# Trainium2, one core: projection passes handed from TensorE to ScalarE one token tile at a time, and a reordered start, in a hybrid RWKV-7 and gated-DeltaNet block

## Chip, cores and metric

The kernel runs on one core of one Trainium2 chip. The metric is the device time of one launch in microseconds (us). The engines are named as the profile names them: PE is TensorE, ACT is ScalarE, DVE is VectorE, POOL is GpSimd and SP is SyncE, which only issues DMAs here.

## What is computed

The layer works on x of 256 tokens by 2048 channels in float32. Its reference, cut to what matters:

```python
xn = rmsnorm(x, norm_mix_pre)
p = (xn @ w_in).astype(f32)
p_rwkv, p_qkv, p_z, p_beta, p_alpha, p_gate_a, p_gate_b = _split(p, IN_SPLITS)
# RWKV-7 branch: 32 heads x 64; its decay, its a and its gate come from three
# narrow ("LoRA") parts of p, 448 columns in all
y_a = (groupnorm(rwkv7_recurrence(...)) + bonus) * out_gate
# gated DeltaNet branch: 16 heads x 128, causal convolution, chunks of 64 frames
y_b = rmsnorm(gated_delta_rule_chunked(q, k, v, g, beta)) * silu(z)
mixed = sigmoid(p_gate_a) * y_a + sigmoid(p_gate_b) * y_b
x = x + rmsnorm(mixed @ w_out, norm_mix_post)
return x + rmsnorm((silu(xn2 @ ffn_w_gate) * (xn2 @ ffn_w_up)) @ ffn_w_down)
```

`w_in` has 2048 rows, and about 18,900 columns; all its products are needed in float32 accuracy.

## The kernel before

**Arithmetic.** Each large product is done in three matmuls: activations and weights are split into a high part that the matmul takes exactly and the rest. `product` issues hi x hi, lo x hi and hi x lo (L285 to L287). ACT makes the high part of a weight piece (`split_hi`, L275, tile `hi_all`), DVE the difference (`split_lo`, L280, tile `lo_all`). A piece of weights of 2 x 128 rows is called a quantum; four quanta are buffered (`QBUF`). PE says `quantum_done` at its end, and ACT may then overwrite the buffer.

**Stages.** The prologue turns x (8 groups of four transposes, L480, through PSUM to `xh` and `xl`, L490 and L500), and multiplies each group at once with the 480 LoRA and beta columns (`project_lora`, 16 quanta of 128 rows). Beside it ACT takes the squares for the first norm; its reciprocal root `rx` scales every accumulator that is emptied. Behind the projection stand the small steps for the LoRA parts, among the first splits of unit 0. Then come 16 units, one for each pair of RWKV heads and one DeltaNet head. A unit needs 24 quanta: three passes of eight quanta, each with 384 columns and all 16 row blocks, accumulated in PSUM banks 6 (tokens 0 to 127, tile 0) and 7 (tokens 128 to 255, tile 1). `take_out` (ACT, L311, tile `pu`) empties both banks, scaled by `rx`; then PE may begin the next pass, for which it waits for `pass_out`.

**Order of the work.** There is no scheduler. Each engine has a list that is written out by hand, and `fill(n)` puts the next n quanta (on ACT and DVE: their splits) between the steps of the recurrences. In a unit those steps are, in order: chunk work of the unit before, the small products for this one, then a triangular solve in levels (`LV`), each with a block Y and a block X of small 32-row matmuls (L984, tile `xs`, `yc`, `xi`), for which DVE prepares `yc` and `xi` (L1435). The passes of a unit begin behind chunk work, behind block X0 and behind block X4. Semaphores join the lists; an engine executes its list strictly in order.

**Last unit.** Instead of the next unit's projection the fillers are partial products with `w_out`: `out_hi`, `out_lo` (L375, L382), `out_part_pe` (L399 to L401, 344 or 336 columns, 7 quanta for a pass, six passes), emptied by `take_part` (L425, tile `keep`/`part`). Behind them the last two row blocks are added, then the output norm and the feed-forward stage (L530 to L546), which the change leaves alone.

## Time and profile before

| | |
|---|---|
| time before, median of 3 runs | 2151.61 us (2151.55 to 2154.91) |
| the profiled execution | 2157.32 us, its span 2155.6 us |
| mean granted clock of TensorE in it | 0.993 |
| PE busy | 2085.8 us, 97% |
| DVE busy | 1425.1 us, 66% |
| ACT busy | 1093.4 us, 51% |
| POOL busy | 160.4 us, 7% |

All rows below are of this one execution; its own time is the one to hold a sum of its durations against. In the page, a busy PE counts matmuls that overlap, so that a group's durations can add up to more than the stretch that they fill; the distance between the starts of two matmuls is their pace. "Idle before" in a timeline is the time in which the engine did nothing just before the row, with what ended it.

### The profile page before, as it was taken

What the parts mean: (1) busy time and instruction counts of PE and PEld (TensorE: products, weight loads), DVE (VectorE), ACT (ScalarE), POOL (GpSimd) and SP (SyncE); (2) the same over time, 40 slices, a digit from 0 to 9 for tenths busy, and PEclk for the clock granted to TensorE, in tenths of its full rate; (3) what the DMA queues carried; (4) which work ended last, traced back from release to release, by engine and by line L of the source; (5) the groups of instructions that cost most, each with busy time, mean ns of one, the idle gap of its engine ahead of it and who ended that gap; (6) DMA issues with size and microseconds to landing.
All of it is one profiled execution on the core that took longest, in us unless ns stands there. A gap on an engine that the chain in (4) does not pass through costs nothing. (4 is left out here: it accounts for less than half of the span.)

```text
span 2155.6 us, 49352 instructions
## 1 busy us (share of the span) xinstructions
PE 2085.8 (97%) x20516; PEld 1799.6 (83%) x20516; DVE 1425.1 (66%) x2865; ACT 1093.4 (51%) x2061; POOL 160.4 (7%) x277
## 2 busy tenths in 40 slices
PE   8999999999999999999999999799999999999998
PEld 7888888888888888888888888778888888888886
DVE  5668777777877877877787784764454544554446
ACT  5555554655655555465565554444444444444444
POOL 3001011011011101101101110000000000000000
PEclk9999999999999999999999999899999999999999
DMA  8654445544545444454444524555555555555543
GB/s 241 157 143 121 124 128 135 137 123 124 135 121 143 123 123 125 126 147 125 125 124 122 140 96 138 195 163 189 188 182 194 186 184 192 163 191 195 190 178 138
DMA packets 387773, 327.29 MB, mean 152 GB/s; under 512 B 11792, under 2 KB 334336, under 8 KB 381440
## 3 DMA queue, kind: packets, MB, share of 16 engines
q1 hardware_dynamic: 375792, 319.16, 50.5%
q10 hardware_dynamic: 11792, 5.42, 1.0%
q8 instruction: 142, 2.33, 0.5%
q14 instruction: 47, 0.39, 0.1%
HBM read 322.45 MB, written 2.10 MB: 151 GB/s over the span
## 5 line engine op out<-in xcount | busy, mean ns | idle before, releaser
L285 PE MATMUL ps<-hi_all,xh 128*128 128x384 f32 (+1 forms) x1568 | 562.6, 359 | 28.0 <-ACT pu L311 21.9
L534 DVE TENSOR_TENSOR lo_all<-stage,hi_all 128x1024 fp32r<-128x1024 f32 x263 | 322.1, 1225 | 366.4 <-ACT hi_all L530 366.0
L287 PE MATMUL ps<-hi_all,xl 128*128 128x384 f32 (+1 forms) x1568 | 530.1, 338 | 0.0
L286 PE MATMUL ps<-lo_all,xh 128*128 128x384 f32 (+1 forms) x1568 | 528.6, 337 | 0.0
L530 ACT ACTIVATE hi_all<-stage 128x1024 fp32r<-128x1024 f32 x260 | 275.4, 1060 | 402.4 <-PE ps L546 401.6
L280 DVE TENSOR_TENSOR lo_all<-stage,hi_all 128x768 fp32r<-128x768 f32 (+1 forms) x400 | 377.7, 965 | 117.0 <-ACT hi_all L275 116.3
L275 ACT ACTIVATE hi_all<-stage 128x768 fp32r<-128x768 f32 (+1 forms) x400 | 325.7, 833 | 196.2 <-PE ps L287 188.7
L285 PEld LDWEIGHTS ps<-hi_all,xh 128*128 128x128 f32 x1568 | 295.0, 188 | 63.6 <-issue 27.7
L286 PEld LDWEIGHTS ps<-lo_all,xh 128*128 128x128 f32 x1568 | 295.8, 189 | 0.8
L287 PEld LDWEIGHTS ps<-hi_all,xl 128*128 128x128 f32 x1568 | 295.3, 188 | 1.1
L542 PE MATMUL ps<-hi_all,xh 128*128 128x512 f32 x704 | 277.9, 395 | 5.2 <-DVE xl L500 5.2
L546 PE MATMUL ps<-hi_all,xl 128*128 128x512 f32 x704 | 276.6, 393 | 0.0
L544 PE MATMUL ps<-lo_all,xh 128*128 128x512 f32 x704 | 275.9, 392 | 0.0
L542 PEld LDWEIGHTS ps<-hi_all,xh 128*128 128x128 f32 x704 | 132.6, 188 | 42.5 <-DVE xl L500 6.8
L546 PEld LDWEIGHTS ps<-hi_all,xl 128*128 128x128 f32 x704 | 132.7, 188 | 29.1
L544 PEld LDWEIGHTS ps<-lo_all,xh 128*128 128x128 f32 x704 | 132.8, 189 | 23.4
L542 PE MATMUL ps<-hi_all,hh 128*128 128x512 f32 x348 | 137.8, 396 | 0.0
L544 PE MATMUL ps<-lo_all,hh 128*128 128x512 f32 x348 | 137.5, 395 | 0.0
L546 PE MATMUL ps<-hi_all,hl 128*128 128x512 f32 x348 | 137.4, 395 | 0.0
L1444 DVE SCALAR_TENSOR_TENSOR early<-ps,up,early 128x255 f32<-128x255 f32 (+1 forms) x192 | 83.2, 475 | 1.9
L984 PEld LDWEIGHTS ps<-late 128*64 128x64 f32 (+1 forms) x960 | 52.9, 135 | 32.2 <-issue 28.3
L542 PEld LDWEIGHTS ps<-hi_all,hh 128*128 128x128 f32 x348 | 65.2, 187 | 16.8 <-issue 0.9
(281 smaller groups left out, 2664.3 us busy)
## 6 DMA issues: line engine op xcount, KB each, us to landing
stage<-in_w_in SPq DMA_DIRECT2D x288, 512.0 KB, 5.7
stage<-in_ffn_w_gate SPq DMA_DIRECT2D x44, 1024.0 KB, 5.1
stage<-in_ffn_w_up SPq DMA_DIRECT2D x44, 1024.0 KB, 5.1
stage<-in_ffn_w_down SPq DMA_DIRECT2D x22, 2048.0 KB, 7.6
stage<-in_w_out SPq DMA_DIRECT2D x16, 344.0 KB, 4.3
stage<-in_w_out SPq DMA_DIRECT2D x8, 516.0 KB, 4.5
stage<-in_w_in SPq DMA_DIRECT2D x8, 448.0 KB, 6.3
stage<-in_w_out SPq DMA_DIRECT2D x8, 336.0 KB, 4.7
```

The source lines that it names most:

```text
L275: nc.scalar.activation(split_of(hi, u, q), raw_quantum(u, q), ACT.Copy).then_inc(hi_ready, 1)
L280: nc.vector.tensor_tensor(split_of(lo, u, q), raw_quantum(u, q), split_of(hi, u, q).bitcast(F32), ALU.subtract).then_inc(lo_ready, 1)
L285: nc.tensor.matmul(o, xh[:, kc, xs], high, start=kc == 0, stop=False)
L286: nc.tensor.matmul(o, xh[:, kc, xs], low, start=False, stop=False)
L287: return nc.tensor.matmul(o, xl[:, kc, xs], high, start=False, stop=kc == KC - 1)
L530: nc.scalar.activation(whi[b], src, ACT.Copy).then_inc(ffn_hi, 1)
L534: nc.vector.tensor_tensor(wlo[b], src, whi[b].bitcast(F32), ALU.subtract).then_inc(ffn_lo, 1)
L542: nc.tensor.matmul(o(t), left_hi[:, k, xs], whi[b][:, k, :], start=first and k == 0, stop=False, skip_group_check=True)
L544: nc.tensor.matmul(o(t), left_hi[:, k, xs], wlo[b][:, k, :], start=False, stop=False, skip_group_check=True)
L546: last = nc.tensor.matmul(o(t), left_lo[:, k, xs], whi[b][:, k, :], start=False, stop=False, skip_group_check=True)
L984: return nc.tensor.matmul(o, l, r, start=start, stop=stop, skip_group_check=True)
L1444: steps.step(name, nc.vector.scalar_tensor_tensor(o, x, s, y, op0, op1))
```

## The change

- **Token tile outside, row block inside.** `project` and `out_pe` had the row blocks (`k`) outside and the token tiles (`t`) inside. Now `t` is outside, so that in the last quantum of a pass bank 6 is complete six matmuls before bank 7. PE says so with a new semaphore, `bank_done`. `take_out` and `take_part` empty tile 0 behind `bank_done` and tile 1 behind `quantum_done`, and each of the two instructions adds one to `pass_out`. PE waits for tile 0's before the first matmul of the new pass and for tile 1's before the seventh.
- **Place of the take-outs.** Behind X0 (`i == 0`) the take-out stands ahead of a unit's `fill(before_y[0])` instead of behind it. `take_part` follows the split of quantum `n % OG == 1` instead of `== 2`. In unit 0, the take-out of pass 1 follows split 18 instead of 17.
- **Loads.** The first x load of 512 columns becomes two of 256, the first LoRA weights come in two halves with a semaphore `first_in`, and unit 0's first weights (`load_unit_weights(sp, 0, (0,))`) are issued ahead of `load_small`.
- **First norm.** Two squares of 2048 columns become eight of 512 (`sq0` to `sq7`), one ahead of each group's splits; DVE adds up the eight sums (`sum`).
- **Head of PE.** 24 transposes of the identity into bank 6 (`warm`, 10, 8 and 6) stand ahead of the first norm transpose, ahead of group 0's transposes and behind them. The transposes of group 1 follow quantum 0 and no longer precede it.
- **LoRA steps.** The steps behind the projection (`un`, `shift`, `tlw` and so on) stand at other places among unit 0's splits, and two quanta rather than four precede the LoRA transposes.

The diff, cut to its core:

```diff
--- before.py
+++ after.py
+WARM = (10, 8, 6)
...
-        def load_unit_weights(sp, u):
-            for i in range(6):
+        def load_unit_weights(sp, u, parts=range(6)):
+            for i in parts:
...
+        def landed(fill):
+            return 48 * (fill // 3 + 1) - (32 if fill % 3 == 0 else 0)
...
+        def taken(n, t):
+            return 2 + NT * n + t + 1
         def project(pe, u, q):
             j = q // 8
-            if q % 8 == 0 and not (isinstance(u, int) and u + j == 0):
-                pe.wait_ge(pass_out, 3 * u + (2 + j))
             pe.wait_ge(lo_ready, count(u, q + 1))
-            for k in range(2):
-                for t in range(NT):
+            for t in range(NT):
+                if q % 8 == 0 and u + j > 0:
+                    pe.wait_ge(pass_out, taken(3 * u + j - 1, t))
+                for k in range(2):
                     last = product(ps[:, 6 + t, 0:PW], 2 * (q % 8) + k, t, hi[q % QBUF][:, k, :], lo[q % QBUF][:, k, :])
+                if q % 8 == 7 and t == 0:
+                    last.then_inc(bank_done, 1)
             last.then_inc(quantum_done, 1)
...
             act.wait_ge(quantum_done, QALL + (n + 1 - QBUF))
             nc.scalar.activation(hi[n % QBUF][:, :, 0:OW[out_pass(n)]], out_quantum(n), ACT.Copy).then_inc(hi_ready, 1)
-            if n % OG == 2 and n > OG:
+            if n % OG == 1 and n > OG:
                 take_part(act, n // OG - 1)
...
         def take_out(act, u, j):
-            act.wait_ge(quantum_done, count(u, 8 * (j + 1)))
             for t in range(NT):
-                last = nc.scalar.activation(pu[:, t, (j % 3) * PW:(j % 3 + 1) * PW], ps[:, 6 + t, 0:PW], ACT.Copy,
-                                            scale=rx[:, t:t + 1])
-            last.then_inc(pass_out, 1)
-        def pass_columns(u, j):
-            return 3 * u + (3 + j)
+                if t == 0:
+                    act.wait_ge(bank_done, 3 * u + j + 1)
+                else:
+                    act.wait_ge(quantum_done, count(u, 8 * (j + 1)))
+                nc.scalar.activation(pu[:, t, (j % 3) * PW:(j % 3 + 1) * PW], ps[:, 6 + t, 0:PW], ACT.Copy,
+                                     scale=rx[:, t:t + 1]).then_inc(pass_out, 1)
...
         def take_part(act, p):
-            act.wait_ge(quantum_done, QALL + OG * (p + 1))
             b = part_bank(p)
-            nc.scalar.activation(part[:, :, OAT[p]:OAT[p] + OW[p]], ps[:, b:b + NT, 0:OW[p]], ACT.Copy).then_inc(pass_out, 1)
+            for t in range(NT):
+                if t == 0:
+                    act.wait_ge(bank_done, 3 * NU + p + 1)
+                else:
+                    act.wait_ge(quantum_done, QALL + OG * (p + 1))
+                nc.scalar.activation(part[:, t, OAT[p]:OAT[p] + OW[p]], ps[:, b + t, 0:OW[p]], ACT.Copy).then_inc(pass_out, 1)
...
                     load_x(0)
-                    for fill in range(4):
-                        if fill == 1:
-                            load_x(1)
-                        if fill == 2:
-                            load_x(2)
-                            load_x(3)
-                        if fill >= 3:
+                    load_low(0, 0, 2, 0, 448, first_in)
+                    load_low(0, 0, 4, 448, LW, first_in)
+                    load_x(1)
+                    load_low(0, 2, 4, 0, 448, weights_in[0])
+                    load_x(2)
+                    for fill in range(1, 4):
+                        if fill == 3:
                             load_rows()
                             sp.wait_ge(lo_ready, 4 * fill - 8)
-                        for at, col, n in ((0, COL_LORA, 224), (224, COL_LORA + 224, 224), (448, COL_BETA, 32)):
-                            to = raw[fill % 3].rearrange("p a b -> p (a b)")[:, 0:4 * LW]
-                            sp.dma_start(to.rearrange("p (k n) -> p k n", k=4)[:, :, at:at + n],
-                                         w_in3[:, 4 * fill:4 * fill + 4, col:col + n]
-                                         ).then_inc(weights_in[fill % 3], 16)
+                        for c1, c2 in ((0, 224), (224, 448), (448, LW)):
+                            load_low(fill, 0, 4, c1, c2, weights_in[fill % 3])
+                        if fill < 3:
+                            load_x(fill + 2)
+                    load_unit_weights(sp, 0, (0,))
                     load_small()
-                    load_unit_weights(sp, 0)
+                    load_unit_weights(sp, 0, range(1, 6))
...
+                    def squares(i):
+                        t, c = i % 2, i // 2
+                        act.wait_ge(x_in[max(c + 1, 1)], 16)
+                        if i >= 4:
+                            act.wait_ge(A.sem, A.after(f"sq{i - 4}"))
+                        cs = slice(512 * c, 512 * c + 512)
+                        A.step(f"sq{i}", nc.scalar.activation(junk[:, 512 * (i % 4):512 * (i % 4) + 512], xt[:, t, cs], ACT.Square,
+                                                              accum_out=ssc[:, t, c:c + 1]))
                     for g in G8:
                         if g == 0:
                             act.wait_ge(D_.sem, D_.after("n1"))
+                        else:
+                            squares(g - 1)
                         transpose_x_act(act, A, Pe, NORM1, (g,))
                         for q in (2 * g, 2 * g + 1):
                             split_hi(act, None, q)
-                        if g >= 6:
-                            squares(g - 6)
+                    squares(7)
                     for q in range(2):
...
+                    dve.wait_ge(A.sem, A.after("sq7"))
+                    step("sum", nc.vector.tensor_reduce(ss[:], ssc[:], AX.X, ALU.add))
+                    step("var", nc.vector.tensor_scalar(ss[:], ss[:], 1.0 / D, NORM_EPS, ALU.mult, ALU.add))
+                    root(nc, dve, D_, "rx", rx[:], ss[:], rt[:])
+                    for q in range(2):
+                        split_lo(dve, 0, q)
                     dve.wait_ge(small_in, 16 * N_SMALL)
                     for i, (_, n) in enumerate(lora_cols):
...
+                    def warm(n):
+                        for _ in range(n):
+                            nc.tensor.transpose(ps[:, 6, 0:P], ident[:], ident[:])
                     pe.wait_ge(masks_made, 3)
+                    warm(WARM[0])
...
+                    warm(WARM[1])
                     turn_x(0)
+                    warm(WARM[2])
                     for g in G8:
-                        if g + 1 < KC // 2:
+                        if 0 < g < KC // 2 - 1:
                             turn_x(g + 1)
                         for q in (2 * g, 2 * g + 1):
                             pe.wait_ge(D_.sem, D_.after(f"lo{g}"))
                             project_lora(pe, q)
+                            if q == 0:
+                                turn_x(1)
...
-                    for q in range(4):
+                    for q in range(2):
...
                 for i in LV:
+                    if i == 0 and more:
+                        take_out(act, u, 3)
                     fill(before_y[i])
                     if i == 4:
                         after(E, "Y4")
                         fn("yw", yw[:].rearrange("p a j -> p (a j)"), ps[:, 2, 0:6 * BK])
                     fill(before_x[i])
-                    if i == 0 and more:
-                        take_out(act, u, 3)
```

**First place: ACT at the pass that begins behind X0, in a steady unit.** `th` is the last step of the small products, `hi_all` a split, and `pu` the take-out. Before:

```order
L1300 ACTIVATE th<-pu 128x768
L275 ACTIVATE hi_all<-stage 128x768 [waits quantum_done,weights_in0] x2
L311 ACTIVATE pu<-ps,rx 128x384 [waits quantum_done]
L311 ACTIVATE pu<-ps,rx 128x384
L275 ACTIVATE hi_all<-stage 128x768 [waits quantum_done,weights_in0]
L275 ACTIVATE hi_all<-stage 128x768 [waits quantum_done,weights_in1] x4
```

and in the changed kernel:

```order
L1352 ACTIVATE th<-pu 128x768
L285 ACTIVATE hi_all<-stage 128x768 [waits quantum_done,weights_in0]
L330 ACTIVATE pu<-ps,rx 128x384 [waits bank_done]
L330 ACTIVATE pu<-ps,rx 128x384 [waits quantum_done]
L285 ACTIVATE hi_all<-stage 128x768 [waits quantum_done,weights_in0] x2
L285 ACTIVATE hi_all<-stage 128x768 [waits quantum_done,weights_in1] x4
```

The take-out now has one split ahead of it and not two, and its two instructions wait for two events, not for one.

**PE where such a pass begins,** in a unit of the changed kernel: the last small matmul ahead, then one quantum.

```order
L1036 MATMUL ps<-rhg,xit 64x128
L295 MATMUL ps<-hi_all,xh 128x384 [waits pass_out,lo_ready]
L296 MATMUL ps<-lo_all,xh 128x384
L297 MATMUL ps<-hi_all,xl 128x384
L295 MATMUL ps<-hi_all,xh 128x384
L296 MATMUL ps<-lo_all,xh 128x384
L297 MATMUL ps<-hi_all,xl 128x384
L295 MATMUL ps<-hi_all,xh 128x384 [waits pass_out]
L296 MATMUL ps<-lo_all,xh 128x384
L297 MATMUL ps<-hi_all,xl 128x384
L295 MATMUL ps<-hi_all,xh 128x384
L296 MATMUL ps<-lo_all,xh 128x384
L297 MATMUL ps<-hi_all,xl 128x384
```

Six matmuls on tile 0 stand between the two waits for `pass_out`. Before the change the first row carried the only wait, and the tiles alternated every three matmuls.

**Second place: ACT in the last unit, at the take-out of part 0** (`keep`), before:

```order
L375 ACTIVATE hi_all<-stage 128x2x344 [waits quantum_done,weights_in0] x2
L1300 ACTIVATE late<-ps,ege 128x128 [waits pe_front]
L1300 ACTIVATE late<-ps,ege 128x128
L1300 ACTIVATE late<-ps 128x256 [waits pool_front]
L1300 ACTIVATE late<-ps 64x2x64 x4
L1300 ACTIVATE late<-ps,uh 128x128 x2
L1300 ACTIVATE th<-pu 128x768
L563 DMA g2s<-in_rwkv_g 128x2x128 [waits pe_back]
L375 ACTIVATE hi_all<-stage 128x2x344 [waits quantum_done,weights_in0]
L425 ACTIVATE keep<-ps 128x2x344 [waits quantum_done]
```

and in the changed kernel:

```order
L389 ACTIVATE hi_all<-stage 128x2x344 [waits quantum_done,weights_in0] x2
L447 ACTIVATE keep<-ps 128x344 [waits bank_done]
L447 ACTIVATE keep<-ps 128x344 [waits quantum_done]
L1352 ACTIVATE late<-ps,ege 128x128 [waits pe_front]
L1352 ACTIVATE late<-ps,ege 128x128
L1352 ACTIVATE late<-ps 128x256 [waits pool_front]
L1352 ACTIVATE late<-ps 64x2x64 x4
L1352 ACTIVATE late<-ps,uh 128x128 x2
L1352 ACTIVATE th<-pu 128x768
L586 DMA g2s<-in_rwkv_g 128x2x128 [waits pe_back]
L389 ACTIVATE hi_all<-stage 128x2x344 [waits quantum_done,weights_in0]
```

The take-out has moved ahead of `late`, `th`, the issue of the load of `g2s`, and one split.

**Third place: PE's head**, before:

```order
L836 MATMUL ps<-ident,junk 128x16 [waits norm_in,masks_made]
L480 MATMUL ps<-ident,xt 128x128 [waits x_in0]
L480 MATMUL ps<-ident,xt 128x128 x7
L285 MATMUL ps<-hi_all,xh 128x480 [waits lo_ready,pre_dve]
L286 MATMUL ps<-lo_all,xh 128x480
L287 MATMUL ps<-hi_all,xl 128x480
L285 MATMUL ps<-hi_all,xh 128x480
L286 MATMUL ps<-lo_all,xh 128x480
L287 MATMUL ps<-hi_all,xl 128x480
```

and in the changed kernel:

```order
L879 MATMUL ps<-ident 128x128 [waits masks_made]
L879 MATMUL ps<-ident 128x128 x9
L884 MATMUL ps<-ident,junk 128x16 [waits norm_in]
L879 MATMUL ps<-ident 128x128 x8
L503 MATMUL ps<-ident,xt 128x128 [waits x_in0]
L503 MATMUL ps<-ident,xt 128x128 x3
L879 MATMUL ps<-ident 128x128 x6
L295 MATMUL ps<-hi_all,xh 128x480 [waits lo_ready,pre_dve]
L296 MATMUL ps<-lo_all,xh 128x480
L297 MATMUL ps<-hi_all,xl 128x480
L295 MATMUL ps<-hi_all,xh 128x480
L296 MATMUL ps<-lo_all,xh 128x480
L297 MATMUL ps<-hi_all,xl 128x480
L503 MATMUL ps<-ident,xt 128x128 [waits x_in1]
```

Fillers (L879, whose only input is the identity) stand ahead of and behind the norm's transpose, and once more behind the first group's; the other four transposes of the eight have moved behind quantum 0.

## Rows read from the trace of the kernel before

**Rows 1.** Windows, one unit: us, busy and (count) per engine, PEclk, DMA share, GB/s.
```profile
200.86:278.12 77.26, 75.53 (x1032) 66.95 (x1033) 59.52 (x146) 42.98 (x99) 8.93 (x13) 1.00 0.50 129
```

**Rows 2.** Waits of the whole span: us in total, times, longest us.
```profile
ACT hi_all L275 <- PE ps L287: 188.7, 129, 2.2
...
PE ps L285 <- ACT pu L311: 21.9, 32, 1.1
```

**Rows 3.** Timeline of PE at X0: start us, us, engine, line, operation, tiles, [idle before].
```profile
199.60 0.59 PE L984 MATMUL ps<-yc,xs 32*32 32x16 f32 x48
200.86 0.44 PE L285 MATMUL ps<-hi_all,xh 128*128 128x384 f32 x1 [0.66 <-ACT pu L311]
...
205.70 0.33 PE L287 MATMUL ps<-hi_all,xl 128*128 128x384 f32 x1
205.88 0.33 PE L285 MATMUL ps<-hi_all,xh 128*128 128x384 f32 x1
...
208.05 0.59 PE L984 MATMUL ps<-yc,xs 32*32 32x16 f32 x48
208.57 0.44 PE L285 MATMUL ps<-hi_all,xh 128*128 128x384 f32 x1
```

**Rows 4.** Timeline of ACT and of DVE in the same stretch.
```profile
199.04 0.83 ACT L275 ACTIVATE hi_all<-stage 128x768 fp32r<-128x768 f32 x1
199.78 1.03 ACT L311 ACTIVATE pu<-ps,rx 128x384 f32<-128x384 f32 x2
...
206.29 0.25 DVE L1435 TENSOR_TENSOR yc<-ps,lev 128x96 f32<-128x96 f32 x1
```

**Rows 5.** Timeline of PE behind X4 of the same unit.
```profile
224.49 0.45 PE L285 MATMUL ps<-hi_all,xh 128*128 128x384 f32 x1 [0.65 <-ACT pu L311]
```

**Rows 6.** Timeline of the head on PE, ACT; then windows of it (same columns as the unit).
```profile
5.37 1.97 PE L480 MATMUL ps<-ident,xt 128*128 128x128 f32 x8 [1.25 <-DMA xt<-in_x]
9.60 0.74 PE L285 MATMUL ps<-hi_all,xh 128*128 128x480 f32 x1 [2.26 <-DVE lo_all L280]
...
18.40 0.84 ACT L490 ACTIVATE xh<-ps,par 128x256 fp32r<-128x256 f32 x2 [1.21 <-PE ps L480]
...
9.60:15.08 5.48, 5.48 (x16) 4.53 (x17) 2.42 (x5) 1.36 (x4) 4.40 (x16) 1.00 1.08 379
15.08:18.12 3.04, 3.04 (x20) 2.65 (x18) 1.88 (x4) 1.83 (x4) 2.46 (x9) 1.00 0.80 234
19.27:20.71 1.44, 1.44 (x8) 1.26 (x7) 1.44 (x4) 0.95 (x2) 1.17 (x5) 1.00 0.27 35
```

**Rows 7.** Around 39 and 55 us: PE's waits (30:42, 50:60), ACT, SP, a window.
```profile
PE ps L285 <- DVE lo_all L280: 2.9, 2, 2.3
...
PE ps L285 <- DVE lo_all L280: 0.9, 2, 0.5
...
37.03 1.57 ACT L275 ACTIVATE hi_all<-stage 128x768 fp32r<-128x768 f32 x2 [1.90 <-DMA stage<-in_w_in]
...
26.60 0.43 SPq L248 DMA_DIRECT2D stage<-in_w_in  x1
...
38.80:42.20 3.40, 3.09 (x10) 3.12 (x11) 2.76 (x4) 2.37 (x4) 0.00 (x0) 0.50 1.01 280
```

**Rows 8.** Timeline of PE at the end of pass 0 of unit 0.
```profile
59.45 0.34 PE L287 MATMUL ps<-hi_all,xl 128*128 128x384 f32 x1
60.93 0.44 PE L285 MATMUL ps<-hi_all,xh 128*128 128x384 f32 x1 [1.14 <-ACT pu L311]
```

**Rows 9.** Last unit: window of ACT's work, timeline of ACT, of DVE.
```profile
1275.99:1279.18 3.19, 3.19 (x26) 2.90 (x26) 2.06 (x6) 3.09 (x11) 1.11 (x2) 1.00 0.93 330
...
1280.93 0.74 ACT L425 ACTIVATE keep<-ps 128x688 f32<-128x688 f32 x1 [0.97 <-PE ps L401]
...
1290.33 0.25 DVE L1435 TENSOR_TENSOR yc<-ps,lev 128x96 f32<-128x96 f32 x1
```

More of the change, by code:

```diff
@@ L389, in last_bank, with out_pe @@
             return (6, 0, 2)[p % 3]
-        def out_pe(pe, n, bank, kc0, first):
+        def out_pe(pe, n, bank, kc0, first, emptied=None, tell=False):
             pe.wait_ge(lo_ready, QALL + n + 1)
             w = OW[out_pass(n)]
-            for k in range(2):
-                kc = kc0 + k
-                for t in range(NT):
+            for t in range(NT):
+                if emptied is not None:
+                    pe.wait_ge(pass_out, taken(emptied, t))
+                for k in range(2):
+                    kc = kc0 + k
                     xs, o = slice(t * P, (t + 1) * P), ps[:, bank + t, 0:w]
@@ L401, in out_pe @@
                     last = nc.tensor.matmul(o, xl[:, kc, xs], h, start=False, stop=False, skip_group_check=True)
+                if tell and t == 0:
+                    last.then_inc(bank_done, 1)
             last.then_inc(quantum_done, 1)
@@ L865, in _ @@
                     Pe.step("lora", last)
[L866 removed]
+                    for q in range(2, FIRST):
                         project(pe, 0, q)
```

79 lines of the change are left out of this document (42 added, 37 removed).

## Prediction

> **What bounds the kernel now.** I read the busy shares first, then who waited for whom, then stretches of the timeline. TensorE (PE) is busy for 75.53 us of a unit of 77.26 us, VectorE (DVE) for 59.52, ScalarE (ACT) for 42.98, at the full granted clock [rows 1]. So PE sets the pace of the 16 units. ACT even waits 188.7 us in all for PE to free a split buffer [rows 2], which means that the weight splits run ahead. What PE loses there is mostly one wait: its first matmul of a pass waits for ACT to empty the two accumulators of the pass before, 21.9 us in 32 waits [rows 2]. Two of 1.14 us come before the units (the one at 60.93 [rows 8], and its like 18 us later); the other 30, 19.6 us, are two in each of 15 units: at the passes that begin behind the small blocks X0 and X4. The other parts of the change lie in the first 80 us, where PE stands still several times, and in the last unit with the output projection, where PE follows DVE.
>
> **Part 1, passes handed over by token tile, units 0 to 14.** At the first place the 48 small matmuls of X0 start at 199.60 and the pass at 200.86; behind the same block at 208.05 the next quantum starts at 208.57 [rows 3]. So 1.26 us stand against 0.52: 0.73 us are lost (0.66 idle, and 0.07 of overlap that a stopped PE does not have). ACT shows why: it splits from 199.04 to 199.8, begins the two evacuations at 199.78 when the old pass has just ended, and needs 1.03 us for both [rows 4]. At the second place the pass starts with 0.65 idle behind it [rows 5]; by the same overlap I take 0.71. After the change tile 0 is complete six matmuls (6 x 0.17 = 1.04 us) before the pass ends, so ACT can take it at once; its take-out has also been moved ahead of the split. It is free about 199.1, and empties tile 0 until 199.7, before X0 is over at 200.1. Tile 1 is complete at 199.7 and empty at about 200.3; PE wants it only after the new pass's first six matmuls, at 201.2. Both waits vanish: 15 x (0.73 + 0.71) = **-21.6 us**.
>
> What is late next: the split moved behind the take-out comes at about 200.3 instead of 199.04, and DVE's difference for it about 0.3 us later than now. DVE works in order, so `y1` at 206.29 [rows 4] becomes 206.6 to 206.85, and PE, now 0.73 earlier, asks for it at 207.3 (208.05 less 0.73). 0.4 us of slack remain, so the move costs nothing. The third hand-over of a unit lies behind chunk work and shows no wait now. One increment and one wait more per pass cost nothing that I can find: between 205.70, the last matmul of one quantum (with an increment), and 205.88, the first of the next (with a wait already met), lie 0.18 us, against 0.17 between any two [rows 3]. The Trainium skill (page TensorE: Matmul & The Clock Gate, section The cost: per-tile semaphore tail) speaks against this part: every increment on completion costs about 26 ns and they serialize, so one on the last matmul is better. By that figure some 54 more increments on TensorE would be an estimated 1.4 us against me, and the forecast a good 1 us later; the row's 0.01 us decides.
>
> **Part 2, the first 80 us.** Five things, in order of time.
> (a) Head. The first projection matmul starts at 9.60 and the next group at 15.08, 5.48 us for 16 instructions; no less work takes 3.04 from 15.08 to 18.12 [rows 6]. The granted clock reads 1.00 in both, but its first record in this trace comes only at 14.9; by the times, the first stretch ran at 1.2 GHz and the second at 2.4. The change fills the idle head with 24 transposes. If they bring the full clock by 9 us, the first group needs 2.6 to 3.0 us. But group 1's transposes now come behind quantum 0, and from their end ACT needs 0.84 and DVE, behind it, 1.44 [rows 6], less some overlap, so PE waits for that chain about 1.2 us. The first matmul itself I put at 9.3: x arrives earlier, but ahead of its transposes stand 18 fillers at the pace of the first transposes, 8 in 1.97 us [rows 6]. Group 1 then starts at about 13.4, **-1.6 us** (bounds 0 and -2.4).
> (b) Squares. ACT's two squares of 2,048 columns stand among the last groups' splits; of the 2.9 us that PE waits for DVE there in two waits [rows 7], the shorter one of about 0.5, at 34 us, is theirs, 0.7 lost with the overlap. In eight pieces they fit into the 1.21 us that ACT waits in a group [rows 6]: -0.7.
> (c) First pass. The longer wait, 2.3 us, ends at 39.1 [rows 7], 2.5 lost. DVE waits for a split that ACT can start only at 37.03, since its weights land late; SP issued them at 26.60, behind the small loads [rows 7]. Now they are issued ahead of those, about 6 us earlier, and should have landed long before. What remains is the norm: last square, sum, some ten small DVE operations of the root (0.2 us each, an estimate), one difference. By that I get 0.9 us idle: **-1.6**.
> (d) Clock. Behind that stop the granted clock is 0.50, 1.2 GHz, from 38.8 to 42.2 [rows 7], while PE does 10 matmuls in 3.09 us, 0.31 each where 0.17 is the pace at the full clock [rows 3]: some 1.5 us for what falls into it. With 0.9 us idle I expect no fall: **-1.5**.
> (e) The LoRA steps spread among the splits: PE waits 0.9 us for DVE in two places from 50 to 60 [rows 7], 1.3 with the overlap, and both go. The two pass ends ahead of the units (59.45 to 60.93 is 1.48 in place of 0.17 [rows 8]) cost 1.31 each and go as in part 1: -1.3 - 2.6.
> Together -1.6 - 0.7 - 1.6 - 1.5 - 1.3 - 2.6 = **-9.3 us** (bounds: -4 if (a), (c) and (d) give nothing, -11).
>
> **Part 3, last unit and output projection.** Here the change also costs. `take_part` follows `out_hi` one quantum earlier. For part 0 that puts it ahead of 3.19 us of ACT work (`late` to `th`, 11 instructions from 1275.99) [rows 9], and it must wait for the partial pass to end, which lets ACT evacuate at 1280.93 now [rows 9]. That work then starts at about 1281.4, after the evacuation (0.74 less what tile 0 had in advance); the splits behind it and the squares come 3 to 5 us late. DVE's differences wait for them, then its chain of small operations, then `y1`, which I put at 1292.75, 2.4 later than its 1290.33 [rows 9]; PE wants it at about 1291, by its own pace (an estimate, as is the rest of this part). I charge +2.2 and give back 0.3 for the pass's own wait: **+1.9**. Part 4's take-out now stands between two splits, not behind both, so DVE's last output chain starts about 1.2 later, and part 5's stands ahead of one more split that the last turned tile waits for: +1.2 and +0.6, near the length of one evacuation and of one split. Nothing hides these, as PE waits for DVE there already. Sum **+3.7 us** (bounds 0, if later work has slack, and +6, if the granted clock falls once more at (d)'s price). The feed-forward stage is untouched and PE-bound.
>
> **Sum.** -21.6 - 9.3 + 3.7 = -27.2 us, from the profiled execution's own 2157.3 (span 2155.6 and 1.7 around it): 2130.1. That execution is 5.7 above the median of the three timed runs; I take the saving off the median: 2151.6 - 27.2 = 2124.4, rounded **2124 us**.
>
> **Rivals.**
> - *Fillers do not raise the clock.* Now 8 transposes in 1.97 us from 5.37 [rows 6] left it low, which speaks for it; against it, PE stood still for 2.26 us behind them [rows 6], and the fillers leave no such gap. Then (a) gives nothing or 0.3: 2124.4 + 1.5 = 2126. Chance 0.25. The Trainium skill has that rule (page TensorE: Matmul & The Clock Gate, section Part 4: PE-mode transpose): the full clock does not engage for PE-mode transposes.
> - *ACT does not reach the second tile in time.* Tile 1's 0.57 us plus hand-over latency leave 0.3 us of room; if one of the two hand-overs per unit keeps its wait: + 15 x 0.7 = 2135. Chance 0.07.
> - *DVE binds as soon as PE's wait is gone.* DVE is busy 77% of a unit and its chains set X and Y. Then only part 2 stays: 2151.6 - 9.3 + 3.7 = 2146. Against it: DVE waits for ACT, and ACT for PE, all through. Chance 0.04. That is also the case in which the change does not do what it says.
> - *Slower.* ACT, in order, stands at `bank_done` ahead of the split in every unit as it does in the last one, the difference comes late, `y1` later, and PE waits at X1. It decides once the split is late by more than the 0.4 us of slack plus the 1.8 us a unit that the rest saves (27/15). At 3.2 us late, as in the last unit: (3.2 - 0.4) x 15 = +42, 2166. But ACT reaches the take-out at 199.04, after tile 0 is complete and 0.7 before tile 1 is. Chance 0.02.
>
> **How the numbers follow.** Forecast 0.62, with its own range 2118 to 2130 from the bounds of parts 2 and 3; the rivals 0.25, 0.07, 0.04, 0.02. The range 2115 to 2133 takes in the first rival, the bounds, and the 3.4 us between the timed runs; about 0.15 lie outside. A difference of 0.2% (4.3 us) is about what this kernel's runs can tell from none. Faster 0.96, same 0.02, slower 0.02.
>
> **What would show it.** In a unit of the new profile, no idle PE ahead of the pass behind X0 and behind X4, and units of 75.8 us instead of 77.26. In the head, matmuls 0.22 apart from the first on; no 0.50 clock near 39; the second pass's start at about 53 instead of 60.93. In the last unit, ACT idle ahead of its first `keep` evacuation and PE idle ahead of X1. The prediction is wrong if units keep a wait for `pu`, or if a wait for `lo_all` or `yc` takes its place.

## Result and profile after

The changed kernel takes 2129.24 us (median of 4 runs, 2128.61 to 2130.34) against 2153.26 us of the kernel before (4 runs, 2151.55 to 2155.59). The ratio is 0.9888, 95% interval 0.9871 to 0.9905: 24 us faster, where 27 were forecast. The time itself, 2129.24, is 5.2 us above the 2124 of the forecast: 3.2 of them are the smaller saving, and the rest is mostly the kernel before, whose median is 2153.26 here and was 2151.61 there. A later measurement of the same kernel on another chip (e11 below) gave 2127.04 against 2154.07, a ratio of 0.9878 (0.9862 to 0.9895).

The page and the whole span's waits of PE after the change (us in total, times, longest us):

```profile
span 2126.9 us, 49422 instructions
PE 2081.5 (98%) x20540; PEld 1798.8 (85%) x20540; DVE 1424.9 (67%) x2866; ACT 1097.5 (52%) x2079; POOL 160.8 (8%) x277
```
```profile
PE ps L1036 <- issue: 10.0, 20, 1.2
PE ps L503 <- DVE keep L2059: 6.5, 1, 6.5
PE ps L565 <- DVE xl L523: 5.2, 5, 2.1
PE ps L295 <- DVE lo_all L290: 3.9, 3, 2.0
PE ps L415 <- DVE xl L1325: 3.0, 1, 3.0
PE ps L415 <- DVE lo_all L396: 2.1, 2, 1.4
...
```

PE's wait for `pu` [rows 2] is not in the list any more; all 32 of them are gone. The first row, idle time of PE at the small blocks for which the profile names no releaser, was 7.3 us in 15 waits before. Most of it is 0.42 us at one later block of a unit, in both kernels at the same place (16.6 us behind the pass at X0); the largest new one is the 1.25 us in the last unit shown below. The unit reads like this now, as a window and at block X0, on PE and on ACT (columns as in rows 1 and 3):

```profile
191.56:267.34 75.78, 75.36 (x1041) 66.93 (x1033) 59.50 (x145) 43.17 (x99) 8.93 (x13) 1.00 0.51 131
```
```profile
191.04 0.59 PE L1036 MATMUL ps<-yc,xs 32*32 32x16 f32 x48
191.56 0.44 PE L295 MATMUL ps<-hi_all,xh 128*128 128x384 f32 x1
...
190.48 1.25 ACT L330 ACTIVATE pu<-ps,rx 128x384 f32<-128x384 f32 x2
```

From the start of X0 to the pass behind it 0.52 us go by, as at an ordinary quantum, where it was 1.26 [rows 3]. ACT takes the first tile at 190.48, ahead of X0, where it began as the old pass ended [rows 4]. A unit takes 75.78 us instead of 77.26 [rows 1]: 1.48 each.

The two traces can be laid side by side at the same instructions. The table shows how much earlier the changed kernel reaches each, by its start in either trace.

| reached | before | after | earlier by | in this stretch |
|---|---|---|---|---|
| quantum 2 of the LoRA projection | 15.08 | 15.23 | -0.15 | head (a): -0.15 |
| last LoRA quanta (group 7) | 33.95 | 33.54 | 0.41 | squares (b): 0.56 |
| first pass | 39.11 | 37.66 | 1.45 | first pass (c): 1.04 |
| second quantum of it | 42.70 | 39.84 | 2.86 | clock (d): 1.41 |
| second pass | 60.93 | 55.39 | 5.54 | LoRA steps and a hand-over (e): 2.68 |
| third pass | 79.01 | 72.06 | 6.95 | a hand-over: 1.41 |
| first output quantum behind the last take-out of a unit | 1256.97 | 1227.65 | 29.32 | 15 units: 22.4 |
| block Y4's quantum in the last unit | 1296.69 | 1269.42 | 27.27 | part 0's take-out: -2.05 |
| third output quantum behind it | 1306.10 | 1277.02 | 29.08 | a clock fall that only the trace of before has: 1.81 |
| last output quantum | 1383.41 | 1356.90 | 26.51 | parts 4 and 5: -2.57 |
| end | 2155.6 | 2126.9 | 28.7 | clock falls that lie otherwise: 1.25; gathered from 1400 to 1800 without a fall: 0.97 |

The two profiled executions lie 28.7 us apart, the medians 24.0. The clock of these two does not tell why in total: both have a mean granted clock of 0.993, and about 31 us at 0.50 each. What differs is where the falls lie. Two of the kernel before have no like in the other trace (3.4 us from 38.8 and from 1301.7), the changed kernel has one in the head (3.4 us from 9.5) and a longer one near 1344 (6.8 us, where the kernel before has 3.4), and the fall of 10.2 us behind the output projection is in both, but in the changed kernel more of it lies where PE stands idle (before, then after):

```profile
1390.50:1400.70 10.20, 7.95 (x24) 6.21 (x25) 7.41 (x17) 1.68 (x4) 0.00 (x0) 0.50 0.30 92
```
```profile
1361.20:1371.40 10.20, 5.05 (x15) 3.98 (x16) 9.56 (x33) 3.06 (x7) 0.00 (x0) 0.50 0.04 3
```

The trace alone with all these effects taken out says about 27 us. That is an estimate: 28.7, less 1.4, 1.8 and 1.25 for the falls that cost the kernel before more, plus 1.2 for the longer fall near 1344 and 1.7 for the one in the head (15.23 there, 13.54 in e11).

A median mixes executions of different clocks, and the time of one kernel follows its mean granted clock. Thirteen runs of the kernel before on one chip took 2149.94 to 2152.91 us at a mean clock of 0.995 or 0.996 (five runs), 2153.89 to 2156.50 at 0.993 or 0.994 (seven) and 2158.96 at 0.992. Held against each other at one clock, the two kernels lie 26 to 28 us apart at 0.993 (four of these runs, and the two of the changed kernel at 2128.61 and 2129.11, on another chip), and on e11's chip 24.4 to 26.4 at 0.994 and about 26.5 at 0.995. So the change is worth some 24 to 28 us, and the runs do not tell a 27 from a 25.

In the head, the transposes and the start of the projection, and the clock in two windows there:

```profile
4.29 1.94 PE L879 MATMUL ps<-ident 128*128 128x128 f32 x8
6.05 0.62 PE L503 MATMUL ps<-ident,xt 128*128 128x128 f32 x4
6.50 0.82 PE L879 MATMUL ps<-ident 128*128 128x128 f32 x6
9.30 0.58 PE L295 MATMUL ps<-hi_all,xh 128*128 128x480 f32 x1 [1.98 <-DVE lo_all L290]
...
15.23 0.45 PE L295 MATMUL ps<-hi_all,xh 128*128 128x480 f32 x1 [0.62 <-DVE lo_all L290]
```
```profile
6.00:9.00 3.00, 1.32 (x12) 1.08 (x10) 1.29 (x3) 2.23 (x5) 2.50 (x8) 1.00 1.01 353
9.50:12.50 3.00, 3.00 (x11) 2.49 (x10) 0.26 (x1) 0.00 (x0) 2.37 (x9) 0.50 1.12 372
```

Eight fillers take from 4.29 to 6.05, 0.22 us each; the four transposes behind them and the next fillers are 0.11 apart. So the full clock came at 6.0 us, by transposes alone, 8.9 us earlier than before (14.9). Then PE stood still for 1.98 us, and from 9.5 on the granted clock is 0.50 (1.2 GHz) for more than 3 us. The first six matmuls run at the low clock again, and in this execution nothing is won.

In the last unit, ACT at the take-out of part 0 and PE at block X1:

```profile
1250.66 0.46 ACT L447 ACTIVATE keep<-ps 128x344 f32<-128x344 f32 x1 [3.90 <-PE ps L417]
1251.61 0.46 ACT L447 ACTIVATE keep<-ps 128x344 f32<-128x344 f32 x1 [0.49 <-PE ps L417]
1251.96 0.62 ACT L1352 ACTIVATE late<-ps,ege 128x128 f32<-128x128 f32 x2
```
```profile
1262.97 0.58 PE L1036 MATMUL ps<-yc,xs 32*32 32x16 f32 x48 [1.25 <-issue]
```

ACT waits 3.90 us for the first tile, with `late` and `th` behind it in its list. They start at 1251.96; in the place that they had before [rows 9] they would have started at 1275.99 less 29.32, that is 1246.67. The price shows up 11 us later, where PE waits 1.25 us. That row names no releaser; that the wait comes from the take-out's place is shown by e3 below.

### The profile page after: what moved, and what is told of

Read it like the earlier page. It is cut to its first block and busy times, and to the rows that moved or that the text cites. A ratio compares the mean times of both kernels' runs of the same rounds, so it can differ in the third digit from the quotient of the medians.

```text
span 2126.9 us, 49422 instructions
## 1 busy us (share of the span) xinstructions
PE 2081.5 (98%) x20540; PEld 1798.8 (85%) x20540; DVE 1424.9 (67%) x2866; ACT 1097.5 (52%) x2079; POOL 160.8 (8%) x277
## 5 line engine op out<-in xcount | busy, mean ns | idle before, releaser
L295 PEld LDWEIGHTS ps<-hi_all,xh 128*128 128x128 f32 x1568 | 294.2, 188 | 36.1 <-issue 24.4
L569 PEld LDWEIGHTS ps<-hi_all,xl 128*128 128x128 f32 x704 | 132.4, 188 | 28.7
```

The lines of the kernel that those rows point to most:

```text
L295: nc.tensor.matmul(o, xh[:, kc, xs], high, start=kc == 0, stop=False)
L569: last = nc.tensor.matmul(o(t), left_lo[:, k, xs], whi[b][:, k, :], start=False, stop=False, skip_group_check=True)
```

## Experiments

Times are medians; each ratio is to the kernel before, with its 95% interval. The runs of one group (e1 to e4, e5 to e8, e9 to e11) shared a chip; the changed kernel itself was timed beside none but e9 and e10, as e11. Across groups, 2 to 3 us between two versions are not told apart by medians, so there the traces are read.

| run | us | ratio | interval |
|---|---|---|---|
| changed kernel | 2129.2 | 0.9888 | 0.9871 to 0.9905 |
| e1 hand-over only | 2131.4 | 0.9894 | 0.9878 to 0.9911 |
| e2 start only | 2150.4 | 0.9982 | 0.9971 to 0.9992 |
| e3 parts late | 2121.8 | 0.9850 | 0.9833 to 0.9867 |
| e4 order kept | 2131.5 | 0.9899 | 0.9882 to 0.9915 |
| e5 no fillers | 2127.7 | 0.9878 | 0.9862 to 0.9895 |
| e6 filled gap | 2127.0 | 0.9874 | 0.9858 to 0.9891 |
| e7 both tiles wait | 2139.1 | 0.9932 | 0.9915 to 0.9948 |
| e8 first difference | 2128.2 | 0.9883 | 0.9867 to 0.9900 |
| e9 combined | 2122.5 | 0.9852 | 0.9836 to 0.9869 |
| e10 new head | 2126.5 | 0.9874 | 0.9858 to 0.9891 |
| e11 changed again | 2127.0 | 0.9878 | 0.9862 to 0.9895 |
| e12 two edits | 2124.6 | 0.9867 | 0.9850 to 0.9883 |

**e1, the hand-over alone, and e2, the start alone.** e1 is the kernel before with the edits of `project`, `take_out`, `out_pe`, `take_part` and the moved take-outs behind X0 and of the parts; e2 has all the others.

> The kernel before with the hand-over by token tile alone (all passes, the moved take-outs too), its start unchanged. Theory A, the parts add up as the two traces show them: 15 units x 1.49 = 22.4 us, two pass ends ahead of the units 2.6, against 4.6 us lost in the last unit and the output projection: about 20 us faster than before (range 17 to 23), units of 75.77 us. Theory B, the earlier start is needed for it (splits of unit 0 that run ahead): units stay above 76 us and less than 15 us are gained.

> The kernel before with the new start alone (loads, squares, fillers, LoRA steps), passes handed over as before. Theory A: 7.1 us of the first 118 less the 2.6 that the two pass ends there cost gives 4.4 us faster (3 to 6), with the 0.50 clock near 40 us gone. Theory B, what is won at the start is taken back by a wait for the first pass ends (their take-outs now stand behind more steps): under 2 us.

e1 gained 23.5 us, with units of 75.78 us in its trace, and e2 4.4 us, with PE's wait for `pu` still there (21.6 us in 32). Theory A holds for both, and they add up to 27.9, a little more than the whole change gives. Neither part needs the other. e1 was to gain 20 (range 17 to 23) and gained 3.5 more, just outside the range. What makes up the difference is open. Its trace tells one thing about the clock: it has the same stop ahead of the first pass as the kernel before, even a longer one, yet the clock did not fall behind it. PE there, and the window that read 0.50 before [rows 7]:

```profile
39.44 0.41 PE L286 MATMUL ps<-hi_all,xh 128*128 128x384 f32 x1 [2.96 <-DVE lo_all L281]
```
```profile
38.80:42.20 3.40, 2.76 (x16) 2.79 (x17) 2.76 (x4) 2.70 (x5) 0.00 (x0) 1.00 1.09 292
```

So the 1.4 us of the fall at 39 us come with one execution and not with the other, and the stop alone does not decide. (e1's execution has falls of its own elsewhere, at 1277 and at 1400, and is the slowest of its four.)

**e4, the order on ACT undone, and e7, the tiles handed over together.**

```diff
 e4
                 for i in LV:
-                    if i == 0 and more:
-                        take_out(act, u, 3)
                     fill(before_y[i])
...
                     fill(before_x[i])
+                    if i == 0 and more:
+                        take_out(act, u, 3)
 e7, take_out
-                if t == 0:
-                    act.wait_ge(bank_done, 3 * u + j + 1)
-                else:
-                    act.wait_ge(quantum_done, count(u, 8 * (j + 1)))
+                act.wait_ge(quantum_done, count(u, 8 * (j + 1)))
```

> The changed kernel with the take-out behind X0 put back behind the split, in units 0 to 14. Theory A, both orders are needed: ACT begins the take-out only some 0.7 us later, as the old pass ends, tile 0 is empty 0.3 to 0.4 us after X0, and each unit waits at that place: 0.4 to 0.5 us a unit with the overlap, 5 to 8 us slower than the changed kernel, units of 76.2 us. Theory B, the order of the tiles alone does it: units stay at 75.77 us.

> The changed kernel, where ACT takes tile 0 of a unit's pass only when the whole pass is done (as tile 1), though it still says so for each tile. Theory A, both halves of the hand-over are needed: tile 0 is empty 0.6 to 0.7 us after the pass, block X0 or X4 covers 0.5 of it, so PE waits 0.1 to 0.2 at two places a unit, 0.2 to 0.25 with the overlap: 6 to 8 us slower than the changed kernel, units of 76.2 us. Theory B, it is enough that PE need not wait for tile 1: units stay at 75.8 us.

PE's waits from 190 to 1180 us in e4, the place behind X0 there, and PE's two waits in a unit of e7:

```profile
PE ps L295 <- ACT pu L330: 3.9, 14, 0.3
```
```profile
189.27 0.59 PE L1036 MATMUL ps<-yc,xs 32*32 32x16 f32 x48
190.14 0.41 PE L295 MATMUL ps<-hi_all,xh 128*128 128x384 f32 x1 [0.28 <-ACT pu L330]
...
189.43 1.03 ACT L330 ACTIVATE pu<-ps,rx 128x384 f32<-128x384 f32 x2
```
```profile
192.52 0.41 PE L295 MATMUL ps<-hi_all,xh 128*128 128x384 f32 x1 [0.24 <-ACT pu L327]
215.85 0.41 PE L295 MATMUL ps<-hi_all,xh 128*128 128x384 f32 x1 [0.27 <-DVE lo_all L290]
...
215.12 1.05 ACT L327 ACTIVATE pu<-ps,rx 128x384 f32<-128x384 f32 x2 [0.48 <-PE ps L297]
```

Both are slower than the changed kernel, and theory A has the direction of both. In e4 the wait is 0.28 us each time (0.4 to 0.5 with the overlap had been expected), a unit takes 76.10 us, and the loss is 2 to 5 us, by medians or by the units of the same chip (15 x 0.33), below the 5 to 8 stated. ACT begins the take-out 0.16 us behind the start of X0, where the changed kernel begins it 0.56 us ahead (190.48 and 191.04); X0 hides most of those 0.7 us, since PE wants tile 0 alone. In e7 PE waits at both places. The second row names `lo_all`, but DVE had long been done; ACT's take-out, begun only at 215.12, is what ends the wait, and the row of ACT shows it. A unit takes 76.50 us, and the kernel is about 11 us slower than those of its group with the whole hand-over (2127.0 to 2128.2), more than the 6 to 8 expected: the units' part is about 9 of the 11, and the expectation had left out the two pass ends ahead of the units, which cost another 1.9 (the passes there start 18.64 and 17.65 us apart, where e11 has 17.71 and 16.67). e7 keeps the count for each tile and the order of ACT's list, and with those alone a unit gains somewhat more than half: 0.76 of the 1.48 us by 77.26 and 76.50, or 0.86 of 1.43 against e2's units of 77.36 and e8's of 75.93, which are of e7's kind (see the two levels at the end). The early take of tile 0 gives the rest, and ACT's order is worth what e4 lost. The order of the tiles and the count for each tile were not tested apart.

**e3, the parts' take-outs back at their old place.**

```diff
-            if n % OG == 1 and n > OG:
+            if n % OG == 2 and n > OG:
                 take_part(act, n // OG - 1)
```

> The changed kernel with the take-outs of the output parts one split later, where they were before (n % OG == 2). Theory A, their place is what costs in the last unit: the wait of 1.25 us ahead of block X1 and the 0.7 behind it go, and so do the 0.7 us wait and part of the 3.0 us wait near the end: 3 to 4 us faster than the changed kernel, some 28 us faster than before. Theory B, the two separate evacuations of a part cost it (two of 0.42 us where one of 0.74 was): no difference to the changed kernel.

PE at block X1, and at the first output quantum that needs the last turned tile, in e3:

```profile
1260.02 0.59 PE L1036 MATMUL ps<-yc,xs 32*32 32x16 f32 x48
```
```profile
1341.56 0.43 PE L415 MATMUL ps<-hi_all,xh 128*128 128x344 f32 x1 [2.23 <-DVE xl L1325]
```

The 1.25 us wait is gone, and of the 3.02 us wait 2.23 are left (it was 2.5 before the change). From trace to trace, e3 gains 1.69 us at X1 (0.41 and 1.28), and 0.88 and 0.79 at the two later stops: 3.4, as expected. Clock falls in between go both ways (e3 has one more, at 1271 us, and a shorter one at 1342). The medians say 7.5 between two chips, 5 against e11; what they have above 3.4 no trace shows. Theory A is shown; the two separate evacuations cost nothing that the trace shows.

**e5 and e6, the fillers.**

```diff
-WARM = (10, 8, 6)
+WARM = (0, 0, 0)      (e5)
+WARM = (10, 8, 25)    (e6)
```

> The changed kernel without the 24 filler transposes. Theory A, the fillers bring the full clock before the first projection and it may hold: without them the matmuls from about 9 us on are 0.40 us apart until 13 to 15 us, and group 1 starts at 15 us or later; 0 to 2 us slower than the changed kernel. Theory B, transposes do nothing for the clock: the head reads as in the changed kernel's trace, no difference.

> The changed kernel with 25 fillers behind group 0's transposes in place of 6, so that PE does not stand still for the 2 us ahead of the first projection matmul. Theory A, it is this idle stretch that lets the clock fall at 9.5 us in some executions: it stays at 1.00 from the moment it rises, quantum 0 takes 1.4 us, group 1 starts at 13.3 to 13.6 us, and it does so reliably: 0.5 to 1.5 us faster in the median than the changed kernel. Theory B, transposes do not hold the clock: it falls at about 9.5 us all the same, or quantum 0 starts later by what the fillers take.

PE's head in e5:

```profile
4.18 1.11 PE L503 MATMUL ps<-ident,xt 128*128 128x128 f32 x4
7.94 0.74 PE L295 MATMUL ps<-hi_all,xh 128*128 128x480 f32 x1 [2.64 <-DVE lo_all L290]
...
14.03 0.45 PE L295 MATMUL ps<-hi_all,xh 128*128 128x480 f32 x1 [0.44 <-DVE lo_all L290]
```

and in e6, with the window that read 0.50 in the changed kernel:

```profile
6.79 2.89 PE L879 MATMUL ps<-ident 128*128 128x128 f32 x25
9.61 0.45 PE L295 MATMUL ps<-hi_all,xh 128*128 128x480 f32 x1
...
14.08 0.45 PE L295 MATMUL ps<-hi_all,xh 128*128 128x480 f32 x1 [0.75 <-DVE lo_all L290]
```
```profile
9.50:12.50 3.00, 3.00 (x17) 2.56 (x16) 0.58 (x2) 0.89 (x3) 2.42 (x9) 1.00 1.11 373
```

e5 bears out neither theory as it stands: its matmuls are 0.40 apart until the clock rises at about 12.1, as A says, but group 1 starts at 14.03 and not at 15, and the kernel is not slower. It shows what the fillers cost: without them x's transposes begin at 4.18 instead of 6.05, since 18 fillers at 0.22 us stood ahead of them, and the projection begins at 7.94. e6 holds the clock, as theory A said, but keeps the late start and ends at the same 14.08. Of the eight executions with fillers 10, 8, 6 (the changed kernel twice, e2, e3, e4, e7, e8 and e12), three let the clock fall at about 10 us, with quantum 2 at 15.2 to 15.3; in the five others it held, and quantum 2 came at 13.26 to 14.21. Their mean is 14.2, against 14.03 in the one execution of e5. So the fillers do raise the clock, and no gain from them is seen; three medians of one group within 1.2 us (e5, e6, e8, the last with an edit of its own) say the same. The 0.5 to 1.5 us by which e6 was to beat the changed kernel cannot be told: the changed kernel was not in that group.

**e8, DVE's first difference ahead of the root.**

```diff
+                    split_lo(dve, 0, 0)
                     dve.wait_ge(A.sem, A.after("sq7"))
                     step("sum", nc.vector.tensor_reduce(ss[:], ssc[:], AX.X, ALU.add))
...
-                    for q in range(2):
-                        split_lo(dve, 0, q)
+                    split_lo(dve, 0, 1)
```

> The changed kernel with DVE's first difference of unit 0 ahead of the norm's sum and root, not behind. Theory A, the idle 1.28 us ahead of the first pass is this root chain alone: the first matmul of unit 0 follows the last of group 7 without a wait, 1.3 to 1.4 us faster than the changed kernel up to 70 us. Theory B, the weights land too late or the scaled LoRA block comes late instead: a wait of the same length moves to the first or the third quantum.

PE where group 7 ends and the first pass begins:

```profile
34.22 0.38 PE L297 MATMUL ps<-hi_all,xl 128*128 128x480 f32 x1
34.43 0.34 PE L295 MATMUL ps<-hi_all,xh 128*128 128x384 f32 x1
```

The stop is gone and none takes its place: theory A. Against e4, whose head ran alike (quantum 2 at 13.49 and 13.45), `th` of unit 0 comes 1.40 us earlier. In the median such an amount is not seen.

**e11, the changed kernel again; e10, a head that starts earlier; e9, three edits together.** e10's head:

```diff
-WARM = (10, 8, 6)
+WARM = (10, 0, 8, 11)
...
-                        if 0 < g < KC // 2 - 1:
+                        if g + 1 < KC // 2:
                             turn_x(g + 1)
+                        if g == 0:
+                            warm(WARM[3])
...
-                            if q == 0:
-                                turn_x(1)
```

> The changed kernel itself, once more, on the chip of the two others. Theory A, the difference between executions of one kernel is where the granted clock falls: its head shows quantum 2 at 13.3 to 13.5 us if the clock held at 9.5 us, at 15.2 if it fell, and its other stages repeat the first trace within 0.2 us a unit; 2127 to 2131 us. Theory B, the first trace was an exception: the waits in the last unit (1.25 and 3.0 us) or the units' 75.8 us do not repeat.

> The changed kernel with the new head alone (fillers 10, 0, 8, 11; group 1's transposes ahead of quantum 0). Theory A: first projection matmul at 8.0 to 8.3 us at the full clock, quantum 2 at 10.8 to 11.3 without a wait, 2 to 3 us faster than the changed kernel. Theory B, the loads bind: quantum 2 early but a wait of 1 us or more for x or weights before 20 us, at most 1 us faster.

> The changed kernel with three edits together: the parts' take-outs one split later (as in the run e3), DVE's first difference of unit 0 ahead of the norm's root (as in e8), and a head in which the transposes of group 0 come first thing, those of group 1 ahead of quantum 0, and 29 fillers close the gaps. Theory A, the three lie in different stages and add up: 4 to 5 us from the parts, 1.4 from the difference, 2 to 3 from the head (quantum 2 at about 11 us instead of 13.3 to 15.2): 8 to 10 us faster than the changed kernel, about 2120 us. Theory B, the head is bound by the loads: the gain of the head shows up again as a wait for x or weights between 10 and 20 us, 6 us in all.

e11 bears out theory A: quantum 2 at 13.54, the waits of 1.25 and 3.0 us in their places. e10 has its first projection matmul at 8.61 and quantum 2 at 11.65, a little later than expected, 1.9 earlier than e11. Then the lead is lost, first where ACT waits for the first unit's weights and PE behind it, then once more:

```profile
32.40 0.84 ACT L285 ACTIVATE hi_all<-stage 128x768 fp32r<-128x768 f32 x1 [2.53 <-DMA stage<-in_w_in]
```
```profile
34.89 0.41 PE L295 MATMUL ps<-hi_all,xh 128*128 128x384 f32 x1 [2.09 <-DVE lo_all L290]
45.26 0.44 PE L295 MATMUL ps<-hi_all,xh 128*128 128x384 f32 x1 [0.87 <-DVE lo_all L290]
```

`th` of unit 0 starts at 109.15 in e10, and at 109.15 in e11. Theory B holds in what it says of the loads and of the gain, though the wait lies at 32 us and not ahead of 20: SP's queue issues those weights from 21.87 on, and they have not landed when a faster head asks for them. e9's trace shows the loads binding at two other places: x's second piece landed late, and so did later weights of the first unit, for which ACT and behind it PE wait at 45 to 47 us. A clock fall follows:

```profile
8.60 0.33 PE L503 MATMUL ps<-ident,xt 128*128 128x128 f32 x1 [1.49 <-DMA xt<-in_x]
45.01 0.84 ACT L285 ACTIVATE hi_all<-stage 128x768 fp32r<-128x768 f32 x1 [2.41 <-DMA stage<-in_w_in]
46.97 0.45 PE L295 MATMUL ps<-hi_all,xh 128*128 128x384 f32 x1 [1.77 <-DVE lo_all L290]
```
```profile
48.40:51.80 3.40, 3.40 (x13) 3.40 (x12) 3.23 (x8) 1.86 (x5) 0.00 (x0) 0.50 1.16 297
```

`th` of unit 0 starts only at 112.48 there, 3.3 us behind e11: in this execution, the slowest of e9's four, the faster start has lost more than it won.

By medians e9 as a whole is 4.5 us faster than e11, about what the parts' place alone gives, not the 8 to 10 of theory A.

**e12, the two edits without the new head** (those of e3 and e8).

> The changed kernel with the parts' take-outs one split later and DVE's first difference of unit 0 ahead of the norm's root; the head is the changed kernel's own. Theory A, what held the combined version back is that a faster head runs into the first unit's weights, which land at 32 to 33 us; without it the other two edits add up: no wait ahead of the first pass, no 1.25 us wait in the last unit, 5.5 to 6.5 us faster than the changed kernel, about 2121 us. Theory B, the two do not add up: as fast as the version with the parts late alone or slower.

2124.6 us, 0.9867: faster than the changed kernel of either measurement, but its interval holds the 0.9878 of e11, and e3 with one edit less read 0.9850. Its trace has no stop ahead of the first pass and none at X1; in its head the clock fell (quantum 2 at 15.18), and once more at 1273. By medians, e3, e9 and e12 are one level of 2122 to 2125 us, below both kernels; which of them is best is not settled.

## Why the prediction held, and where it was off

**Part 1** was right in mechanism and size. Both waits vanished, and a unit lost 1.48 us where 1.44 were worked out: 22.4 for 21.6. Both traces are of the lower of the two levels of a unit's time that the last section tells of. The two pass ends ahead of the units gave 1.31 to 1.41 each, priced at 1.31. ACT was done with the second tile at 191.73, and PE's seventh matmul, which needs it, started at 192.71: 1.0 us of room, as part 1's own times say (200.3 and 201.2), and not the 0.3 of the rival on the second tile. The move of the split cost nothing: PE does not wait for `y1` in the units. The Trainium skill's 26 ns for every increment (TensorE: Matmul & The Clock Gate, The cost: per-tile semaphore tail), an estimated 1.4 us, is not seen: the units gained more than forecast, not less. No run measured the increments by themselves.

**Part 2** was forecast at -9.3 and came out at -7.0 in the two traces. The step that came out worst is (a), "Group 1 then starts at about 13.4": in the profiled execution it started at 15.23, and the -1.6 became +0.15. What the step left out is that the clock can fall again while PE waits for the first difference. In five of eight executions it did not, and then the group started at 13.3 to 14.2 (13.54 in e11). The first rival, that fillers do not raise the clock, is refuted by the 0.11 us pace from 6.0 on, in a stretch where PE had done nothing but transposes. The Trainium skill's rule that the full clock does not engage for PE-mode transposes (TensorE: Matmul & The Clock Gate, Part 4: PE-mode transpose), beside which it was set, does not agree with this trace, if `nc.tensor.transpose` is what the page means. The case that happened was in neither the forecast nor the rival: raised, and lost again. (b) gave 0.56 for 0.7. (c) gave 1.04 for 1.6: the root chain left 1.28 us idle, not 0.9 (e8 shows that it is this chain). The argument on the weights, "should have landed long before", was too sure: e10 shows them landing at 32.4, 10.5 us after their issue at 21.87, and the changed kernel's ACT asks for them at 31.68 in e11, 10.9 us after their issue at 20.77. They are just in time. (d) gave 1.41 for 1.5, but e1 shows the stop without the fall, so it should have been priced as a chance. (e) was right: 2.68 with one of the two hand-overs, priced at 1.3 and 1.3. The start of the second pass, named as 53 us in "What would show it", came at 55.39 (53.69 in e11), and the matmuls 0.22 us apart from the first on came in e11 and not in the profiled execution.

**Part 3** was right in place and sign: +2.05 net for +1.9 at part 0, with the wait at X1 as named, and +2.57 for +1.8 at parts 4 and 5, of which only 1.4 are longer stops and 1.2 is a longer clock fall, the case named in its bounds. Together +4.6 for +3.7. Of the stops' 3.4, e3 takes back all.

**The sum** of the stages is -22.4 - 7.0 + 4.6 = -24.8, against -27.2 forecast: part 1 gave 0.8 more, parts 2 and 3 were 2.3 and 0.9 worse. These terms hold the falls of two single executions; with them taken out the traces say about 27, and the medians say 24.0 (first measurement) and 27.0 (e11). That the last of these meets the forecast is in part luck, since terms that were off by 0.6 us, (c), and by a fall that comes or not, (a) and (d), stand against a part 1 that gave more. Of the rivals, those on the second tile, on DVE and "Slower" are excluded for this kernel. e7 and e4 show that a neighbour of the first was near, the wait for the first tile: without the early take of tile 0, or with the take-out behind the split, it comes back at 0.24 to 0.28 us.

## To carry to other kernels

In this kernel the gain came from these steps, and they are worth trying elsewhere. When an accumulator set is handed from one engine to the next and the gap between users is a small block, finish and empty it tile by tile, and put the consumer's instruction ahead of work that can wait; but where the consumer's list is in order and the producer is late, the same move holds up everything behind it (3.90 us of ACT standing at `bank_done`), so choose the place in each stage by when the producer ends there. Here a faster start was worth only what the next loads in the queue allowed (e10, e9): look up when the data behind it land before pricing it. And where the clock can fall, price the fall by its chance and judge by clock-matched runs and by traces, not by one profiled execution.

## What the runs showed of the hardware

- The mean granted clock of an execution of the kernel before told its time within about 3 us, at some 2 us for 0.001 (thirteen runs, 2149.94 to 2158.96 us at 0.996 to 0.992). Where the falls lie matters too: 10.2 us at 0.50 met 7.95 us of busy PE in one trace and 5.05 in another.
- Transposes alone, from 1.75 us on, brought the full clock before the projection: 0.22 us each became 0.11. In the eight executions with the fillers 10, 8, 6 this came at between 5.0 us (e7) and 7.9 us (e3), and at 6.0 in the first trace of the changed kernel. With PE still for 1.98 us behind them, the granted clock fell at 9.5 in that trace and held in another execution of the same kernel (e11).
- Nearly all units of one execution agree within 0.1 us, but executions have two levels: 75.78 us in the changed kernel's first trace, e1, e3 and e10, and 75.9 in e5, e6, e8, e9, e11 and e12, with the same order of work in the units, and with e9, e10 and e11 on one chip. Without the change it is 77.26 in the kernel before and 77.36 in e2. Laid side by side, the small blocks take the same time within 0.02 us a unit; the other 0.15 to 0.19 us lie between the starts of the 288 large matmuls, less than 0.001 us each. Over 15 units that is some 2 us; what sets the level stays open.
